# Weights pass through three raw and four converted buffers instead of five and three

## The reference

```
# first_block: DEPTH = 2, layer 0 is mla, layer 1 is gla
for i in range(DEPTH):
    sx, scx, gx = modulation(c, ada_w[i], ada_b[i])        # silu(cond) @ w + bias
    sc, scc, gc = modulation(c_ctx, ada_w[i], ada_b[i])
    hx = rms_norm(x, norm_g[i]) * (1 + scx) + sx
    hc = rms_norm(ctx, norm_g[i]) * (1 + scc) + sc
    yc, yx = mla_mixer(...) or gla_mixer(...)
    x = x + gx * yx
    if i < DEPTH - 1: ctx = ctx + gc * yc
return rms_norm(x, final_g)
```

## Time and profile before

| | us |
|---|---|
| median of 3 runs | 2039.76 (2034.82 to 2042.78) |
| profiled execution, its own time | 2036.04 |
| its span | 2034.0 |
| PE busy | 1925.4 (95%) |
| DVE busy | 1075.4 (53%) |
| ACT busy | 868.8 (43%) |
| POOL busy | 603.9 (30%) |

### The profile page before, as it was taken

The page is one execution under the profiler, slowest core; times in us unless marked ns, Lnnn a source line. Parts: engine busy times, 40 slices in busy tenths (PEclk is TensorE's granted clock), DMA queues, the critical chain, the costliest instruction groups (busy, mean ns, idle before and its releaser), DMA issues.

```text
span 2034.0 us, 28787 instructions
## 1 busy us (share of the span) xinstructions
PE 1925.4 (95%) x11452; PEld 1554.2 (76%) x11452; DVE 1075.4 (53%) x1503; ACT 868.8 (43%) x1203; POOL 603.9 (30%) x254
## 2 busy tenths in 40 slices
PE   5998999999979999979999999999999999999997
PEld 3887777776867888867747888888788778888885
DVE  5123666766256566786985552354525555513543
ACT  4343565666236555453424442344332344423432
POOL 1321011011211111133324343444444334344433
PEclk8999999999989999999999999999999999999999
DMA  8211211221211112122212332232322222323231
GB/s 304 67 63 39 84 53 54 83 74 43 95 48 55 51 53 63 53 79 67 73 42 75 102 95 92 94 104 93 100 87 93 84 93 86 101 93 104 87 100 52
DMA packets 47219, 166.56 MB, mean 82 GB/s; under 512 B 5488, under 2 KB 5744, under 8 KB 47088
## 3 DMA queue, kind: packets, MB, share of 16 engines
q1 hardware_dynamic: 45360, 162.03, 24.3%
q10 hardware_dynamic: 1728, 2.71, 0.4%
HBM read 162.62 MB, written 2.10 MB: 81 GB/s over the span
## 4 chain that ended last, share of the span: by engine, by line
PE 59%; DVE 6%; ACT 2%; issue 1%; POOL 0%; ACTq 0%; DVEq 0%
PE ps L559 19%; PE ps L561 18%; PE ps L560 18%; DVE wS L1968 1%; PE ps L842 1%; ACT sq L1046 1%; DVE wS L1472 1%; DVE hf L1472 1%; DVE X L1478 1%; DVE Alo L1478 0%; DVE acc L1472 0%; PE ps L775 0%; PE ps L857 0%; PE ps L858 0%; PE ps L859 0%
## 5 line engine op out<-in xcount | busy, mean ns | idle before, releaser
L1456 POOL TENSOR_TENSOR wlo<-raw,whi 128x1024 fp32r<-128x1024 f32 x241 | 588.4, 2455 | 1281.1 <-ACT whi L1028 1281.1
L1028 ACT ACTIVATE whi<-raw 128x1024 fp32r<-128x1024 f32 x251 | 258.2, 1055 | 479.2 <-PE ps L561 469.2
L559 PE MATMUL ps<-Ahi,whi 128*128 128x512 f32 (+1 forms) x784 | 312.0, 398 | 21.3 <-DVE Alo L1478 10.1
L561 PE MATMUL ps<-Ahi,wlo 128*128 128x512 f32 (+1 forms) x784 | 307.5, 392 | 0.0
L560 PE MATMUL ps<-Alo,whi 128*128 128x512 f32 (+1 forms) x784 | 307.0, 392 | 0.0
L559 PEld LDWEIGHTS ps<-Ahi,whi 128*128 128x128 f32 x784 | 149.9, 191 | 58.8 <-issue 12.5
L1472 DVE TENSOR_TENSOR ps<-ps,rstd 128x1024 f32<-128x1024 f32 (+1 forms) x60 | 69.7, 1162 | 215.2 <-PE ps L561 179.7
L560 PEld LDWEIGHTS ps<-Alo,whi 128*128 128x128 f32 x784 | 150.2, 192 | 32.1 <-issue 0.5
L561 PEld LDWEIGHTS ps<-Ahi,wlo 128*128 128x128 f32 x784 | 150.1, 191 | 32.0
L1478 DVE SCALAR_TENSOR_TENSOR cv<-ps,vec,cv 128x511 f32<-128x511 f32 (+1 forms) x176 | 131.9, 749 | 70.4 <-ACT cv L1046 65.7
L559 PE MATMUL ps<-Fhi,whi 128*128 128x512 f32 x416 | 163.9, 394 | 3.5 <-DVE Flo L1472 3.5
(11 more groups left out here) (285 smaller groups left out, 3670.2 us busy)
## 6 DMA issues: line engine op xcount, KB each, us to landing
raw<-in_units SPq DMA_DIRECT2D x299, 512.0 KB, 3.5
X<-in_xT SPq DMA_DIRECT2D x4, 512.0 KB, 9.4
out_xT<-X SPq DMA_DIRECT2D x8, 256.0 KB, 2.1
CX<-in_ctxT SPq DMA_DIRECT2D x4, 256.0 KB, 9.8
acc<-in_rope ACTq DMA_DIRECT2D x1, 384.0 KB, 3.1
gmw<-in_gmw ACTq DMA_DIRECT2D x1, 384.0 KB, 3.1
bs<-in_bs ACTq DMA_DIRECT2D x1, 384.0 KB, 3.7
vec<-in_vec ACTq DMA_DIRECT2D x1, 312.5 KB, 4.6
```

The source lines that it names most:

```text
L559: nc.tensor.matmul(out, sh, mh, start=first, stop=False)
L561: return nc.tensor.matmul(out, sl, mh, start=False, stop=last)
L1028: nc.scalar.activation(whi[:, s % CONV, :], raw[:, c % RAW, :], ACT.Copy).then_inc(sem("whi"), 1)
L1456: nc.gpsimd.tensor_tensor(wlo[:, s % CONV, :], raw[:, plan.unit_at[("split", s)] % RAW, :], whi[:, s % CONV, :].bitcast(fp32), ALU.subtrac ...
```

## The change

```diff
-RAW, CONV = 5, 3
+RAW, CONV = 3, 4
```

## The result

The changed kernel took 2062.43 us (median of 4 runs, 2055.73 to 2074.37), the kernel before 2037.53 us. The ratio is 1.0135, with a 95% interval of 1.0103 to 1.0167: slower by some 27 us (the two medians lie 24.9 us apart, the two profiled executions 23.0). The forecast was 2066 us, and +28 for the sum of its steps.

What follows compares the result with a forecast made beforehand. PE, busy 95% of the span, was taken as the bound. Terms 4.3 + 27 - 2 - 2 + 10 - 9 = +28 gave 2064 us on the profiled execution, 2068 on the median; forecast 2066, range 2044 to 2084.

Steps and rivals of the forecast that it cites:

- The +4.3: Prologue: PE's first product starts near 49.3 instead of about 45.0 us; cost +4.3, range +3 to +6.
- the cadence: Prologue, from the fourth `ada` tile on: latency of a pair of loads sets the pace, about 4.3 us a tile.
- That PE could not catch up: Behind the prologue: PE has no gap from 45 to 175 us in which to recover the +4.3.
- +27: Attention, six pairs of heads: 18 us of PE waits plus 9 of lower clock; bounds +9 to +36.
- The second pair: Attention, second pair of heads: load lands 6.1 us after issue, so PE loses 4.3 us.
- the +2 for dips: Gated linear attention heads: clock dips add 0 to 5 us, taken as 2, within the heads' +10.
- the +1 for a `wlo` beside the tables: Fourth gated linear attention head: one more `wlo` beside DVE's S5 tables costs +1.
- that half: Output, S5, gated MLP: about half of 14.8 us of waits and 4 of dips gained: -9, range -14 to -4.
- Rival C: Feed-forward and short convolution stage: three raw buffers starve it, +160, 2200 us; 0.04 together with other slower cases.
- A: Attention loads arrive in time (within 1.8 us of issue), or PE has other work: faster, 2024 to 2028 us; chance 0.08.
- B: Attention: other PE work hides 1.5 us of each stall, clock stays; +9 there, 2046 to 2050 us; chance 0.16.
- D: Whole kernel: heads cost nothing, mixer gives full 14, gains and losses cancel; 2031 to 2035 us; chance 0.10.

Runs made afterwards that it cites:

- e3_place_only: Kernel before (5 raw, 3 converted buffers) with only the six attention conversions moved to the changed kernel's places, loads still early: 2039.56 us, ratio 1.0009.
- e2_raw4_conv3: Kernel before with four raw buffers instead of five, three converted buffers kept: 2054.64 us, ratio 1.0075.
- e5_six_later: Changed kernel (3 raw, 4 converted buffers) with only the six attention conversions of split units 18 to 23 held eight tiles later: 2038.12 us, ratio 0.9999.
- e1_raw3_conv3: Kernel before with three raw buffers instead of five, three converted buffers kept: 2068.96 us, ratio 1.0154.
- e6_heads_old_place: Changed kernel with the third conversion of each gated linear attention head back at its old place: 2059.86 us, ratio 1.0116.
- e7_heads_pool_later: Changed kernel, ACT's stream untouched, POOL's `wlo` of units 40, 46, 52, 58 held until the head's `lw` tile ended: 2065.28 us in one run.
- e8_both: Changed kernel with the edits of e5_six_later and e6_heads_old_place together: 2035.48 us, ratio 0.9989.
- e9_both_and_tables: e8_both with the conversions of units 60 and 61 also held to the old distance of three: 2031.99 us, ratio 0.9975.
- e10_best: e9_both_and_tables, with unit 60 also waiting for its old tile and split unit 0 loaded before the prologue's last two raw units: 2035.65 us, ratio 0.9998.

## Why the prediction was right

**Prologue: the sum met by luck.** The +4.3 was forecast for PE's first product. That starts at 52.38, where it started at 45.02 before: +7.4. The +4.7 of the table is the last small tile, which no longer waits 4.44 us for DVE. The `ada` tiles follow each other at 4.6 to 5.0 us, forecast 4.3. PE's timeline of the changed kernel, as in the earlier trace rows:

```profile
41.98 1.08 PE L593 MATMUL ps<-raw,cnd 128*32 128x128 f32 x16 [1.78 <-DMA raw<-in_units]
...
46.95 1.08 PE L593 MATMUL ps<-raw,cnd 128*32 128x128 f32 x16 [1.14 <-DMA raw<-in_units]
...
52.38 0.77 PE L559 MATMUL ps<-Hhi,whi 128*128 128x512 f32 x1 [2.56 <-POOL wlo L1456]
```

The step that was wrong is the cadence. It was the landing of the second of two loads, and nothing for PE behind it. In the trace a tile waits for the first of the two loads that are issued when the tile before it ends, because its other unit came with the pair before; this load lands after 3.4 to 3.8 us. Then come 16 matmuls, and they take 1.08 us, as long as 32 of them in the earlier trace rows, where the clock is full: here the granted clock is 0.50 from 32.2 us on, and fell in a wait of PE for a load. By the end of the projections only +4.8 of the +7.4 is left. About 1 us of that comes back because the kernel before is at half clock longer behind its own start (from 45 to 55 us its granted clock is 0.70, from 52 to 60 it is 0.74 in the changed one). Another 1.5 come back at two tiles near the end of the projections: a wait of 0.5 us for DVE's `K` is gone, and the one for DVE's `Q` is 0.7 us instead of 1.3; the rest isn't traced. That PE could not catch up was wrong, and two errors of nearly the same size met.

**Attention: right in place and mechanism, and nearly in size.** 2.4 us of gap forecast in the first pair, 2.55 measured; 18 us in the six, measured 15.9 (16.8 less the 0.9 that was there before). Beside the gaps stand 25.0 - 15.9 = 9.1 us, forecast 9 as six dips of 1.5. There were five dips: the pairs with one lose 1.6 to 1.8 us beside their gap, the fifth 0.5. That is where +27 became +25. e3_place_only, e2_raw4_conv3 and e5_six_later show the cause between them, and that nothing else in attention costs anything.

The second pair was forecast at 4.3, since its load had landed 6.1 us after issue in the trace of before; in the changed kernel's profiled execution the six landed after 4.3 to 4.6, and the longest gap was 2.8. This was luck of that execution. The same load (the second of the two that are issued behind the `ada` tile of the pair), from issue to landing in the twelve traces, in us:

| pair of heads | landed later than 5 us | longest |
|---|---|---|
| first, third, fourth, sixth | in none | 4.6 |
| second | in 7 of 12 traces | 6.5 |
| fifth | in 11 of 12 traces | 5.9 |

So the slow landing belongs to its place after all, and the forecast missed the fifth pair, not the second. Where it comes, the gap grows: 3.8 us in the fifth pair of e1_raw3_conv3, 3.4 to 3.8 in the second and fifth of e6_heads_old_place and e7_heads_pool_later, whose attention costs 27.9 and 27.8 instead of 25.0. Why these two pairs, no run shows.

**End and entry: right.** -2 and -2 forecast, -2.4 and -1.1 measured; e1_raw3_conv3 shows that three raw buffers bring the first.

**Heads: right in mechanism, a third too large.** +10 forecast, +6.9 measured. The stretch of DVE was forecast as 2.2 to 2.4 and was 2.1. The terms that were too large are the +2 for dips (only the first of the four gaps had one, and it has one in the kernel before too) and the +1 for a `wlo` beside the tables: PE already waited for DVE at the end of the fourth head, so what was lost inside it was partly hidden there. e6_heads_old_place shows this from the other side: 7.5 us won in the heads, 4.0 of them given back at line 857. e7_heads_pool_later shows that it is POOL's read against DVE's.

**Output, S5, gated MLP: right sum, other parts.** -9 forecast, -9.5 measured, and e1_raw3_conv3, which has three converted buffers, shows 0.0. The same stretch of the kernel before, then of the changed one:

```profile
884.35:1085.88 201.53, 177.76 (x837) 131.77 (x837) 169.26 (x192) 78.11 (x109) 61.29 (x24) 0.92 0.20 62
```

```profile
917.54:1109.59 192.05, 171.46 (x837) 125.82 (x836) 167.46 (x191) 77.90 (x109) 55.42 (x23) 0.95 0.19 61
```

PE's waits fell by only 3.2 us in sum (23.8 to 20.6). The other 6.3 are busy time: the same 837 matmuls at a higher granted clock. The forecast took 14.8 of waits and 4 of clock and let half through, so the size of that half was a guess that came out. The `wlo` wait of 4.46 and the wait of 4.63 for `X` behind it became one wait of 9.8 for `X`: of the wait nothing was won, as forecast; what went is the stretch at half clock between the two, and the tile behind both gained some 2.5 us. New waits for ACT's `mU` (7.7 us in three) took another part. ACT's timeline there:

```profile
1033.63 0.60 ACT L1046 ACTIVATE mU<-ps 128x512 f32<-128x512 f32 x1 [7.77 <-DVE ps L1472]
...
1042.68 0.60 ACT L1046 ACTIVATE mU<-ps 128x512 f32<-128x512 f32 x1 [3.04 <-DVE ps L1472]
```

ACT isn't late by itself, it waits for DVE. So DVE was late next, as forecast, by way of ACT.

**Feed-forward nets: right.** -0.7, and PE idles 6.9 us there in both kernels. Rival C (starving) left nothing in the trace.

**Rivals.** A fell: no landing was below 3.3 us. B didn't come: nothing was hidden, the gaps were 2.55 to 2.8. D fell with the heads. The direction was decided by the number that rival A named.

**Two slips in the sums.** With 4.3 a tile the eighth `ada` tile ends at 44.9, not 45.2. And the upper bound of attention, with the four other waits as long as the worst, is 2.4 + 5 x 4.3 + 9 = 33, not 36, so the top of the range was 3 us too high. Neither decides anything.

## What to carry to other kernels

- Where a planner places an instruction by "its input's load may be issued now", it places the wait for the load's latency on that engine as well. Add the landing time to the rule (here 4.2 to 6.5 us for the second of two loads of 512 KB; eight tiles covered it), and a shorter ring may cost nothing.
- Ask of every deeper buffer which other engine it starts earlier, and against whom. The fourth converted buffer won 9.5 us in one stage and lost 6.9 in another, where POOL's earlier read met DVE.
- When PE's wait for one engine vanishes, look for the next engine that is late at the same tile, before counting the gain. Then take PE's busy time between two tiles apart from its idle time: of the 9.5 us won here, 6.3 were clock.
- Read a latency that a forecast needs at every place where it comes back, and in more than one execution.

## What the runs showed of the hardware

**Two rates at one granted clock.** Executions of one kernel spread by 15 us or more, and the traces show a reason. The stretch from 1700 to 1850 us in the changed kernel, then in e6_heads_old_place, where PE is busy throughout and its stream is the same (columns as in the earlier trace rows):

```profile
1700.00:1850.00 150.00, 150.00 (x657) 123.05 (x656) 62.33 (x79) 57.30 (x71) 64.61 (x27) 1.00 0.28 92
```

```profile
1700.00:1850.00 150.00, 150.00 (x645) 121.67 (x644) 60.97 (x77) 56.03 (x69) 63.60 (x27) 1.00 0.28 92
```

657 matmuls in one, 645 in the other, 1.8% fewer, and both at a granted clock of 1.00. The matmuls of 512 columns follow each other at 229 ns in the one, at 233 in the other. Such stretches last some 100 to 500 us and lie elsewhere in each execution (from about 1450 to 1550 in the kernel before, from 1100 to 1600 in e5_six_later, from about 1700 on in e1_raw3_conv3 and 1640 in e6_heads_old_place; e2_raw4_conv3 has it in most of the last stage). From the first feed-forward norm to the last product the twelve traces take 903.4 to 918.6 us, and PE idles 5.9 to 6.9 of them in each. The cause is open. It means that single executions differ by 5 to 10 us for no reason of the kernel, and that effects of 3 us are better read from the step between two tiles than from medians. The sums of steps at 1085 us (-8.3 in e8_both, -3.6 in e9_both_and_tables, -5.5 in e10_best) aren't contradicted by the ratios, nor shown by them.

**A gap's size doesn't settle the clock.** In attention, gaps of 1.20 to 1.31 us left the granted clock at 1.00, and those of 2.13 and 2.55 were followed by 3.4 us at 0.51 and 0.54. But the changed kernel's fifth gap of 2.69 us was followed by 1.00, and so were one of 2.47 in e1_raw3_conv3 and one of 2.57 in e6_heads_old_place. And the second head's gap of 2.13 us is the same in the changed kernel and in e5_six_later, and so is the stream around it. The stretch behind it in the one, then in the other:

```profile
739.10:742.50 3.40, 3.38 (x48) 2.29 (x49) 2.28 (x4) 1.72 (x2) 0.00 (x0) 1.00 0.02 5
```

```profile
713.50:716.90 3.40, 3.40 (x43) 1.68 (x44) 1.57 (x3) 0.90 (x1) 0.00 (x0) 0.57 0.02 5
```

In e5_six_later three such gaps were followed by a dip that the changed kernel's profiled execution was spared. That is why its heads cost 11 us and not 7. A dip behind a gap of 2 us is a chance of 1.5 us or so, not a fixed price.
